# Expert weights in pieces of 1024 columns, with four gate/up buffers instead of three

## The chip, the cores and the metric

The kernel runs on one core of one Trainium2 chip. Its time is the device time of one execution in microseconds (us); lower is better. The kernel before took 1544.51 us, the median of 3 runs (1544.26 to 1546.76).

## The reference, cut to what matters

The reference is one step of a two-layer decoder trunk for a prompt of 512 rows and 64 sample rows, 576 rows of 1024 float32 columns in all. Each layer runs three token mixers, merges them, normalises (LN1), and then runs a mixture of experts and a second normalisation (LN2):

```python
D_MODEL = 1024; SEQ = 512; DEPTH = 2; DEC_BATCH = 8; DEC_SEQ = 8
N_EXPERTS = 16; N_EXPERT_GROUPS = 4; TOP_K = 2; D_EXPERT = D_MODEL // 4
# Each layer (DeepNorm post-normalisation, alpha = (2*DEPTH)^(1/4)):
#   x <- LN1(alpha*x + W_out( sum_b sigmoid(G_b x) * P_b(mixer_b(x)) ))   b in {pool, gmlp, nsa}
#   x <- LN2(alpha*x + MoE(x))     (one router shared by all layers; group-limited top-2)
'w_gate': nrm(ks[28], (DEPTH, N_EXPERTS, D_MODEL, D_EXPERT), D_MODEL ** -0.5),
'w_up':   nrm(ks[29], (DEPTH, N_EXPERTS, D_MODEL, D_EXPERT), D_MODEL ** -0.5),
'w_down': nrm(ks[30], (DEPTH, N_EXPERTS, D_EXPERT, D_MODEL), D_EXPERT ** -0.5 * DN_BETA),
```

Every row goes to two of 16 experts. An expert is a gate and an up product (1024 columns to 256 each), a gated activation, and a down product (256 to 1024). Its weights are 2 MB of gate and up (2048 KB) and 1 MB of down (1024 KB), all of them read in every layer.

## The kernel before, in words

The work that the change touches is the expert stage, `experts(k)`, once in each layer, and the end of `merge(k)` ahead of it. The rows of one expert are gathered into chunks of 128 slots. The first 16 chunks are the 16 experts: chunks 0 to 13 are written out (`STATIC = 14`), chunks 14 and up run in a loop of pairs, here one pair, so that chunks 0 to 15 are computed in each layer. A seventeenth chunk's gate/up weights are loaded and prepared but not used.

Five queues work on a chunk n, each in its own written order and bound to the others by semaphores.

- PE (lines 1807 to 1846): `gate_up(n)`, 24 matrix products of 512 columns; `hidden_t(n-1)`; `next_rows_t`, the transposes of the gathered rows of chunk n+1 (L1808); `down(n-1)`, 8 products (L1843).
- ACT: `gate_up_high(n+1)`, four copies of 1024 columns that round the raw gate/up weights to their high part (L1881); then small copies, and `output_copy(n-1)`, which moves the result of a down product to a buffer `y_a` or `y_b` (L1901, L1902).
- DVE: the low part of the same weights, written over the raw ones in place (L2036), and the hidden row.
- POOL: for each chunk an indirect DMA that gathers the rows of a later chunk into `rows_a` or `rows_b` (L1946), and one that adds the result of a chunk to the rows of the tensor `expert_rows` (L1950, here called the scatter). Two scatters may hit one row, so a scatter waits until the one before it has landed. One chunk's instructions stand as: wait for the transposes, gather (four chunks ahead of the scatter), wait for `output_copy`, wait for the scatter before, scatter. POOL's transfers go by the queue q0.
- SP: all weight loads, by the queue q1. A load of gate/up (`load_gu`, L1738) moves 128 rows of 4096 columns, 16,384 bytes each; a load of down (`load_dw`, L1741) 128 rows of 2048 columns, 8,192 bytes each. Both queues run on the same 16 DMA engines.

Three raw gate/up buffers go round (`RING_E = 3`, the number `ch.raw` of a chunk), and three for down (`ch.dslot`). SP loads gate/up of chunk n when `gate_up(n-3)` is finished, and right behind it, when `down(n-4)` is finished, the down weights of chunk n-1. The gate/up weights of the chunks 0 to 2 are issued at the end of `merge(k)` (L1425), ahead of the stores of the normalised rows (L1428, L1429); the down weights of these chunks at the beginning of the expert stage.

The functions that the diff touches, with their line numbers:

Of the kernel before, what the change touches and what calls it, by code (L numbers as in the profile page):

```python
# [14 lines left out]
F32 = mybir.dt.float32  # L15
# [12 lines left out]
KT_D = D // 128  # L28
# [56 lines left out]
def constants():  # L85
# [58 lines left out]
    put("lane", np.tile(r, (128, 1)))  # L144
    put("row1", r + 1)
    put("tile128", np.tile(128 * (np.arange(2 * NTT) % NTT), (128, 1)))
    put("pairgate", np.tile(np.where(np.arange(6) == 0, STATIC - 1, STATIC + 2 * np.arange(6)), (128, 1)))
    put("over", np.tile(128 * (15 - np.arange(16)), (128, 1)))
    spare = np.concatenate([np.zeros(MAXCH + 2), TOK + np.arange(MAXCH + 2)])
    put("pad", np.where(r[:, None] < 127, 8192, spare[None]) + 1)  # L150
# [47 lines left out]
def build(nc, io):  # L198
    with ExitStack() as ctx:
# [46 lines left out]
        for l in range(L):  # L246
            k.layer = l
            LAYER_NAME[0] = f"_{l + 1}" if l else ""
            k.dve, k.act, k.pool = Steps(nc.vector, dve_s), Steps(nc.scalar, act_s), Steps(nc.gpsimd, pool_s)
            k.merge = MergeBuffers(k)  # L250
            with ExitStack() as phase:
                def sp(name, shape, dt=F32):
                    return phase.enter_context(sbuf(nc, name, shape, dt))
                k.z = sp("z", [128, NTT, TM])
                k.qT = sp("qT", [128, GQA, SEQ])
                k.qsT = sp("qsT", [128, B, GQA, TS])
                k.KT = sp("KT", [128, 2, SEQ])
                k.KTs = sp("KT_sample", [128, 2, NS])
                k.kcT = sp("kcT", [128, NKV, 32])
                k.kcsT = sp("kcT_sample", [128, NB - 32])  # L260
                k.vblk = sp("vblk", [128, NKV, GQA, HD])
                k.vcs = sp("vcs", [128, NKV, HD])
                k.gates = sp("gates", [128, NTT, 24])
                k.gsr = sp("gates_by_row", [128, 2, NKV, 3])
                k.small = sp("small", [128, NSMALL])
                k.s = {n: k.small[:, lo:hi] for n, (lo, hi) in _S.items()}
                front(k)
            with ExitStack() as weights:
                k.gu, k.guL = two_types(nc, weights, "gate_up", [128, RING_E, 4096])
                k.dw = weights.enter_context(sbuf(nc, "down", [128, RING_E, 2048], F32))  # L270
            k.guH = [t[:, :, :].rearrange("p a t -> p (a t)")[:, 0:4096] for t in (k.oT_low, k.xT_low)]
            k.gu_in = [sem(f"gate_up_in{n}") for n in range(RING_E)]
            k.dw_in = [sem(f"down_in{n}") for n in range(RING_E)]
            k.w_hi, k.w_lo = sem("gate_up_high"), sem("gate_up_low")
            merge(k)
            experts(k)
            nums = [s.num for s in k.sems]
            assert sorted(nums) == list(range(min(nums), max(nums) + 1))

            nc.gpsimd.dma_reset(range(min(nums), max(nums) + 1))  # L280
            nc.all_engine_barrier(sems_to_clear=range(min(nums), max(nums) + 1))
# [1003 lines left out]
RING_E = 3  # L1285


PIECES = 4
PW = 4096 // PIECES
EARLY = 3  # L1290
# [77 lines left out]
def merge(k):  # L1368
# [16 lines left out]
    with ExitStack() as ctx:  # L1385
# [18 lines left out]
        @block.sync  # L1404
        def _(sp):
            for u in range(FIRST_M, NU):
                if u >= RING + FIRST_M:

                    sp.wait_ge(unit_done, u - RING + 1)
                dst = w32[:, u % RING, 0:width[u]]  # L1410
                if u < NG_:
                    sp.dma_start(dst, io["wm"][l, u // 3, :, UNIT_AT[u % 3]:UNIT_AT[u % 3 + 1]]).then_inc(w_in[u % RING], 16)
                else:
                    kk = 2 * (u - NG_)
                    sp.dma_start(dst.rearrange("p (k n) -> p k n", k=2), io["wo"][l, :, kk:kk + 2, 0:HALF]
                                 ).then_inc(w_in[u % RING], 16)

            sp.wait_ge(unit_done, NG_)
            for q in range(4):
                sp.dma_start(wo32[:, 2 * q:2 * q + 2, :], io["wo"][l, :, 2 * q:2 * q + 2, HALF:D]).then_inc(wo_in[q], 16)  # L1420
            norm.load(sp)

            sp.wait_ge(unit_done, NU)
            for n in range(RING_E):
                sp.dma_start(k.gu[:, n, :], io["we"][l, n, :, 0:4096]).then_inc(k.gu_in[n], 16)  # L1425
            for i, rows in enumerate(TILES):
                sp.wait_ge(norm.ready, 2 * i + 2)
                sp.dma_start(io["x1"][i * 128:i * 128 + rows, :], k.x[0:rows, i, :]).then_inc(x1_stored, 16)  # L1428
                sp.dma_start(io["ys"][i * 128:i * 128 + rows, :], k.x[0:rows, i, :]).then_inc(k.sum_started, 16)  # L1429

        @block.tensor
        def _(pe):
# [74 lines left out]
        def _(act):  # L1507
# [38 lines left out]
            for i in range(NTT):  # L1546
                if i == 2:

                    act.wait_ge(m_done, NTT)
                    act.wait_ge(k.gu_in[0], 16)  # L1550
                    first_expert_high(0)
                norm.copies(act, i)
                if i in (2, 3):
                    first_expert_high(i - 1)
# [87 lines left out]


def fixed_chunk(c):
    return Chunk(c, c % 2, c // 2, c % RING_E, c // RING_E + 1, c % RING_E, c % RING_E, c // RING_E + 1)


def looped_chunk(p, a):

    n, half = p * 2 + (STATIC + a), p + (STATIC + a) // 2  # L1650
    if a % 2:
        return Chunk(n, 1, half, 0, p + (a // 2 + 6), 0, 1, p + (a // 2 + 6))
    return Chunk(n, 0, half, 1, p + (a // 2 + 5), 2, 2, p + (a // 2 + 5))


def experts(k):
# [7 lines left out]
    gu, guL, guH, dw = k.gu, k.guL, k.guH, k.dw  # L1664
# [17 lines left out]
    with ExitStack() as outer:  # L1682
# [5 lines left out]
        with ExitStack() as ctx:  # L1688
# [14 lines left out]
            with ExitStack() as routing:  # L1703
# [12 lines left out]
                slotf = sr("slot_f", [128, 2, NTT])  # L1716
                sloti, lane, chunkno = (sr(n, [128, 2 * NTT], I32) for n in ("slot_i", "slot_lane_i", "slot_chunk_i"))
                C3 = sr("slot_rows", [128, 2 * NTT, 3, NTAB], BF16)
                CW3 = sr("slot_weights", [128, 2 * NTT, 3, NTAB], BF16)
# [4 lines left out]
            y = [sb("y_a", [128, D]), sb("y_b", [128, D])]  # L1724
            xTH, xTL = sb("rowsT_high", [128, KT_D, 128], F32R), sb("rowsT_low", [128, KT_D, 128], F32R)
            block = ctx.enter_context(nc.Block())

# [7 lines left out]
            @block.sync  # L1735
            def _(sp):
                def load_gu(ch, e):
                    sp.dma_start(gu[:, ch.raw, :], io["we"][l, e, :, 0:4096]).then_inc(gu_in[ch.raw], 16)  # L1738

                def load_dw(ch, e):  # L1740
                    sp.dma_start(dw[:, ch.dslot, :], io["we"][l, e, :, 4096:6144]).then_inc(dw_in[ch.dslot], 16)  # L1741
                for n in range(RING_E):
                    load_dw(fixed_chunk(n), n)
                norm.load(sp)
                for n in range(RING_E, STATIC + 1):
                    sp.wait_ge(gu_done, n - RING_E + 1)
                    load_gu(fixed_chunk(n), n)
                    if n > RING_E:
                        sp.wait_ge(dn_done, n - RING_E)
                        load_dw(fixed_chunk(n - 1), n - 1)  # L1750
                with sp.Fori(0, pairs(sp)) as p:
                    even, odd, after = looped_chunk(p, 0), looped_chunk(p, 1), looped_chunk(p, 2)
                    e = [sp.value_load(plan[0:1, bass.ds(ch.n, 1)], min_val=0, max_val=E - 1) for ch in (even, odd, after)]
                    gate = sp.value_load(plan[0:1, bass.ds(p + 34, 1)], min_val=STATIC - 1, max_val=STATIC + 10)

                    sp.wait_ge(gu_done, gate)
                    load_gu(odd, e[1])
# [18 lines left out]
            def _(pe):  # L1776
# [39 lines left out]
                def gate_up(ch):  # L1816
                    out = ps[:, GB + ch.side, :]
                    for kk in range(KT_D):
# [7 lines left out]
                        last = pe.matmul(out, xTH[:, kk, :], guL[:, ch.slot, cols], start=False, stop=(kk == KT_D - 1))  # L1826
                    last.then_inc(gu_done, 1)

                def hidden_t(ch):
# [5 lines left out]
                def down(ch, first=False):  # L1835
# [1 line left out]

                        pe.wait_ge(y_out, ch.n)
                    pe.wait_ge(ht_out, ch.n + 1)
                    pe.wait_ge(dw_in[ch.dslot], ch.d_nth * 16)  # L1840
# [27 lines left out]
            def _(act):  # L1868
# [3 lines left out]
                act.activation(ex[0:NS, NT, :], ps[0:NS, LOGITS, NT * E:NTT * E], ACT.Exp, scale=-1.0).then_inc(ex_ready, 1)  # L1872

                def gate_up_high(ch, early=False, begin=0):
                    act.wait_ge(gu_in[ch.raw], ch.raw_nth * 16)
                    if not early:

                        act.wait_ge(gu_done, ch.n - 1)
                    for q in range(begin, PIECES):
                        cols = slice(q * PW, (q + 1) * PW)  # L1880
                        act.copy(guH[ch.side][:, cols], gu[:, ch.raw, cols]).then_inc(w_hi, 1)  # L1881

                def rows_high(count):
                    act.wait_ge(xt_done, count)
# [104 lines left out]
            def _(dve):  # L1989
# [42 lines left out]
                def gate_up_low(ch, pieces=(0, 1, 2, 3)):  # L2032
                    for q in pieces:
                        cols = slice(q * PW, (q + 1) * PW)
                        dve.wait_ge(w_hi, ch.n * PIECES + (q + 1))
                        dve.tensor_tensor(guL[:, ch.slot, cols], gu[:, ch.raw, cols], guH[ch.side][:, cols].bitcast(F32),  # L2036
                                          ALU.subtract).then_inc(w_lo, 1)


# [366 lines left out]
```

## Time and profile before

| what | value |
|---|---|
| median of 3 runs | 1544.51 us |
| the profiled execution's own time | 1547.95 us |
| its span, first to last instruction | 1546.3 us |
| mean granted TensorE clock | 0.963 |
| PE busy | 1432.9 us (93%) |
| DVE, ACT, POOL busy | 800.9, 612.4, 171.3 us |
| DMA moved | 239.75 MB, mean 155 GB/s |
| expert stage of the first layer | about 560 to 745 us |
| expert stage of the second layer | about 1323 to 1506 us |

Durations and places come from the profiled execution; it lies 3.44 us above the median of the runs. A busy share is the time in which an engine had an instruction; a DMA share is the time in which its 16 engines had packets. PEclk is the clock that TensorE was granted, as a part of full speed. In timelines the first number is the start in us from the beginning of the span, the second the duration, and a bracket gives the idle time ahead of the instruction and what ended it.

### The profile page before, as it was taken

What the parts mean: (1) busy time and instruction counts of PE and PEld (TensorE: products, weight loads), DVE (VectorE), ACT (ScalarE), POOL (GpSimd) and SP (SyncE); (2) the same over time, 40 slices, a digit from 0 to 9 for tenths busy, and PEclk for the clock granted to TensorE, in tenths of its full rate; (3) what the DMA queues carried; (4) which work ended last, traced back from release to release, by engine and by line L of the source; (5) the groups of instructions that cost most, each with busy time, mean ns of one, the idle gap of its engine ahead of it and who ended that gap; (6) DMA issues with size and microseconds to landing.
All of it is one profiled execution on the core that took longest, in us unless ns stands there. A gap on an engine that the chain in (4) does not pass through costs nothing. (4 is left out here: it accounts for less than half of the span.)

```text
span 1546.3 us, 23017 instructions
## 1 busy us (share of the span) xinstructions
PE 1432.9 (93%) x9168; PEld 1166.6 (75%) x9168; DVE 800.9 (52%) x1351; ACT 612.4 (40%) x1156; POOL 171.3 (11%) x152
## 2 busy tenths in 40 slices
PE   7999899999999959989799999999999998799895
PEld 6897665999997846656478966669999976566563
DVE  3224767433333766656842257673333347766565
ACT  3322578322222226656323326772222212465550
POOL 3012000000000112222112210000000001122230
PEclk9999899999999969999899999999999998799997
DMA  8334400322223759997423143021222256599953
GB/s 269 87 124 159 143 2 2 110 80 85 89 69 109 286 187 334 341 317 268 143 109 120 56 169 134 2 76 56 89 75 90 65 202 244 203 342 341 326 173 125
DMA packets 55861, 239.75 MB, mean 155 GB/s; under 512 B 11718, under 2 KB 19796, under 8 KB 45964
## 3 DMA queue, kind: packets, MB, share of 16 engines
q1 hardware_dynamic: 44716, 216.08, 39.0%
q0 software_dynamic: 11040, 22.21, 6.0%
q8 instruction: 73, 1.20, 0.3%
q14 instruction: 32, 0.26, 0.1%
HBM read 224.55 MB, written 34.49 MB: 168 GB/s over the span
## 5 line engine op out<-in xcount | busy, mean ns | idle before, releaser
L1435 PE MATMUL ps<-xT_high,w_high 128*128 128x288 f32 x704 | 208.0, 295 | 0.0
L1436 PE MATMUL ps<-xT_low,w_high 128*128 128x288 f32 x704 | 207.2, 294 | 0.0
L1437 PE MATMUL ps<-xT_high,w_ring_low 128*128 128x288 f32 x704 | 206.3, 293 | 0.0
L1533 ACT ACTIVATE tanh_gate<-ps 128x576 f32<-128x576 f32 x48 | 31.3, 652 | 295.8 <-PE ps L1437 295.8
L1437 PEld LDWEIGHTS ps<-xT_high,w_ring_low 128*128 128x128 f32 x704 | 132.6, 188 | 0.0
L1436 PEld LDWEIGHTS ps<-xT_low,w_high 128*128 128x128 f32 x704 | 132.5, 188 | 0.0
L1435 PEld LDWEIGHTS ps<-xT_high,w_high 128*128 128x128 f32 x704 | 132.1, 188 | 0.0
L1843 PE MATMUL ps<-down,hidT 128*128 128x512 f32 x256 | 118.0, 604 | 4.2 <-ACT hidT L1894 2.4
L1585 DVE SCALAR_TENSOR_TENSOR branch_part<-tanh_gate,ps 128x576 f32<-128x576 f32 x32 | 24.1, 754 | 176.5 <-ACT tanh_gate L1533 176.5
L1327 POOL TENSOR_TENSOR ln_rs<-ln_mv,const 128x1 f32<-128x1 f32 (+1 forms) x20 | 17.5, 873 | 868.7 <-DVE ln_mv L1322 868.7
L557 PE MATMUL ps<-z_w_high_part,oT_low 128*128 128x454 f32 x260 | 97.3, 374 | 8.7 <-DVE z_w_ring_low L1041 8.7
L2036 DVE TENSOR_TENSOR gate_up_low<-gate_up,oT_low 128x1024 fp32r<-128x1024 f32 x66 | 76.5, 1219 | 55.2 <-ACT oT_low L1881 55.2
L1826 PE MATMUL ps<-gate_up_low,rowsT_high 128*128 128x512 f32 x256 | 102.7, 401 | 0.0
L1041 DVE TENSOR_TENSOR z_w_ring_low<-z_w_ring,z_w_high_part 128x908 fp32r<-128x908 f32 (+1 forms) x34 | 34.1, 1006 | 123.1 <-ACT z_w_high_part L871 122.9
L558 PE MATMUL ps<-z_w_ring_low,oT_low 128*128 128x454 f32 x260 | 96.8, 372 | 0.0
L559 PE MATMUL ps<-z_w_high_part,xT_low 128*128 128x454 f32 x260 | 96.8, 372 | 0.0
L2036 DVE TENSOR_TENSOR gate_up_low<-gate_up,xT_low 128x1024 fp32r<-128x1024 f32 x64 | 74.1, 1218 | 43.8 <-ACT xT_low L1881 43.5
L1560 DVE TENSOR_TENSOR w_ring_low<-w_ring,w_high 128x1280 fp32r<-128x1280 f32 (+2 forms) x52 | 79.7, 1533 | 20.4 <-ACT w_high L1517 19.0
L1843 PEld LDWEIGHTS ps<-down,hidT 128*128 128x128 f32 x256 | 47.2, 195 | 52.7 <-issue 52.6
L963 ACT ACTIVATE probs<-ps,row_max 128x128 f32<-128x128 f32 (+4 forms) x152 | 78.7, 532 | 17.8 <-DVE row_max L1182 17.6
L1182 DVE TENSOR_REDUCE row_max<-ps 128x2 f32<-128x1024 f32 (+3 forms) x76 | 60.6, 800 | 41.6 <-PE ps L723 30.2
L1517 ACT CAST w_high<-w_ring 128x1280 fp32r<-128x1280 f32 (+2 forms) x52 | 67.2, 1292 | 15.9 <-PE ps L1437 9.7
(368 smaller groups left out, 3314.5 us busy)
## 6 DMA issues: line engine op xcount, KB each, us to landing
gate_up<-in_we SPq DMA_DIRECT2D x34, 2048.0 KB, 12.2
down<-in_we SPq DMA_DIRECT2D x32, 1024.0 KB, 10.2
w_ring<-in_wm SPq DMA_DIRECT2D x28, 640.0 KB, 4.1
z_w_ring<-in_wtm SPq DMA_DIRECT2D x30, 454.0 KB, 4.1
w_ring<-in_wm SPq DMA_DIRECT2D x16, 768.0 KB, 4.5
w<-in_w SPq DMA_DIRECT2D x2, 2048.0 KB, 8.8
sel_pages<-in_sel_pages SPq DMA_DIRECT2D x32, 128.0 KB, 2.0
win_rows<-in_win_rows SPq DMA_DIRECT2D x2, 2048.0 KB, 8.1
```

Of the source, the lines that this page charges most:

```text
L557: pe.matmul(out, w[0], x[0], start=first, stop=False)
L558: pe.matmul(out, w[0], x[1], start=False, stop=False)
L559: return pe.matmul(out, w[1], x[0], start=False, stop=last)
L963: act.activation(P[:, m % 3, h, 0:w], ps[:, bank + h, 0:w], ACT.Exp, bias=mx[:, m % 3, h:h + 1], accum_out=den[:, m % 3, h:h + 1]).then_in ...
L1435: pe.matmul(out, w[0], x[0], start=first, stop=False)
L1436: pe.matmul(out, w[0], x[1], start=False, stop=False)
L1437: return pe.matmul(out, w[1], x[0], start=False, stop=last)
L1517: act.copy(wh[:, u % HRING, 0:width[u]], w32[:, u % RING, 0:width[u]]).then_inc(w_hi, 1)
L1560: return dve.tensor_tensor(low, src, high.bitcast(F32), ALU.subtract)
L1826: last = pe.matmul(out, xTH[:, kk, :], guL[:, ch.slot, cols], start=False, stop=(kk == KT_D - 1))
L1843: last = pe.matmul(ps[:, YB + n, :], hT[:, f, :], dw[:, ch.dslot, f * D + n * 512:f * D + (n + 1) * 512], start=(f == 0), stop=(f == 1))
L2036: dve.tensor_tensor(guL[:, ch.slot, cols], gu[:, ch.raw, cols], guH[ch.side][:, cols].bitcast(F32), ALU.subtract).then_inc(w_lo, 1)
```

## The change

Every load of expert weights is cut into DMAs of 1024 columns, so that a row of a DMA is 4096 bytes: four DMAs for gate/up, two for down, on the same semaphore, whose waits are for four or two times 16. There is a fourth raw gate/up buffer, `gate_up_d`, and a chunk's buffer is its number modulo four (in the loop 3 and 0 in turn). Gate/up of chunk n is loaded when `gate_up(n-4)` is finished, one chunk earlier than before, and chunk 3's at the end of `merge(k)`, after the stores of the fourth row tile. Down weights still go round three buffers and wait for the same `down`; in SP's order they stand one chunk later relative to gate/up.

```diff
-    put("pairgate", np.tile(np.where(np.arange(6) == 0, STATIC - 1, STATIC + 2 * np.arange(6)), (128, 1)))
+    put("pairgate", np.tile(np.where(np.arange(6) == 0, STATIC - 2, STATIC + 2 * np.arange(6)), (128, 1)))
...
+                weights.enter_context(sbuf(nc, "below_gate_up_d", [128, 8264], F32))
+                fourth, fourth_low = two_types(nc, weights, "gate_up_d", [128, 4096])
+            k.raw = [k.gu[:, n, :] for n in range(RING_E)] + [fourth[:, :]]
+            k.low = [k.guL[:, n, :] for n in range(RING_E)] + [fourth_low[:, :]]
...
+RING_G = 4
+GU_COLS = [slice(n * 1024, (n + 1) * 1024) for n in range(4)]
+DOWN_COLS = [slice(n * 1024, (n + 1) * 1024) for n in range(2)]
+GU_LOADED, DOWN_LOADED = 16 * len(GU_COLS), 16 * len(DOWN_COLS)
...
             for n in range(RING_E):
-                sp.dma_start(k.gu[:, n, :], io["we"][l, n, :, 0:4096]).then_inc(k.gu_in[n], 16)
+                for cols in GU_COLS:
+                    sp.dma_start(k.gu[:, n, cols], io["we"][l, n, :, cols]).then_inc(k.gu_in[n], 16)
             for i, rows in enumerate(TILES):
...
+                if i == NTT - 2:
+                    for cols in GU_COLS:
+                        sp.dma_start(k.raw[3][:, cols], io["we"][l, 3, :, cols]).then_inc(k.gu_in[3], 16)
...
 def fixed_chunk(c):
-    return Chunk(c, c % 2, c // 2, c % RING_E, c // RING_E + 1, c % RING_E, c % RING_E, c // RING_E + 1)
+    return Chunk(c, c % 2, c // 2, c % RING_G, c // RING_G + 1, c % RING_G, c % RING_E, c // RING_E + 1)
...
     if a % 2:
-        return Chunk(n, 1, half, 0, p + (a // 2 + 6), 0, 1, p + (a // 2 + 6))
-    return Chunk(n, 0, half, 1, p + (a // 2 + 5), 2, 2, p + (a // 2 + 5))
+        return Chunk(n, 1, half, 3, p + (a // 2 + 4), 3, 1, p + (a // 2 + 6))
+    return Chunk(n, 0, half, 0, p + (a // 2 + 4), 2, 2, p + (a // 2 + 5))
...
                 def load_gu(ch, e):
-                    sp.dma_start(gu[:, ch.raw, :], io["we"][l, e, :, 0:4096]).then_inc(gu_in[ch.raw], 16)
+                    for cols in GU_COLS:
+                        sp.dma_start(gu[ch.raw][:, cols], io["we"][l, e, :, cols]).then_inc(gu_in[ch.raw], 16)
...
-                for n in range(RING_E, STATIC + 1):
-                    sp.wait_ge(gu_done, n - RING_E + 1)
+                for n in range(RING_G, STATIC + 1):
+                    sp.wait_ge(gu_done, n - RING_G + 1)
                     load_gu(fixed_chunk(n), n)
-                    if n > RING_E:
-                        sp.wait_ge(dn_done, n - RING_E)
-                        load_dw(fixed_chunk(n - 1), n - 1)
+                    if n > RING_G:
+                        sp.wait_ge(dn_done, n - RING_G)
+                        load_dw(fixed_chunk(n - 2), n - 2)
+                sp.wait_ge(dn_done, STATIC - 3)
+                load_dw(fixed_chunk(STATIC - 1), STATIC - 1)
```

SP's order, at the end of `merge(k)` and the beginning of the expert stage of the first layer, before (L1425 and L1738 load gate/up, L1741 down; L1428 and L1429 store the last, 64-row tile):

```order
L1425 DMA gate_up<-in_we 128x4096 [waits unit_done]
L1425 DMA gate_up<-in_we 128x4096 x2
...
L1428 DMA x1_rows<-x 64x1024 [waits ln1_ready]
L1429 DMA expert_rows<-x 64x1024
...
L1741 DMA down<-in_we 128x2048 x3
L1312 DMA ln2_gb<-in_ln 128x2048
L1738 DMA gate_up<-in_we 128x4096 [waits gate_up_done] x2
L1741 DMA down<-in_we 128x2048 [waits down_done]
```

and now (L1438, L1445 and L1757 load gate/up, L1761 down):

```order
L1438 DMA gate_up<-in_we 128x1024 [waits unit_done]
L1438 DMA gate_up<-in_we 128x1024 x11
...
L1445 DMA gate_up_d<-in_we 128x1024 x4
L1441 DMA x1_rows<-x 64x1024 [waits ln1_ready]
L1442 DMA expert_rows<-x 64x1024
...
L1761 DMA down<-in_we 128x1024 x6
L1324 DMA ln2_gb<-in_ln 128x2048
L1757 DMA gate_up<-in_we 128x1024 [waits gate_up_done]
L1757 DMA gate_up<-in_we 128x1024 x3
```

Three loads have become twelve, and four for the fourth buffer stand ahead of the last tile's stores; the first load of the expert stage, which waits for the same first `gate_up`, is now that of chunk 4 instead of chunk 3.

SP's order at the end of the written-out chunks, before the loop's plan is read, before:

```order
L1738 DMA gate_up<-in_we 128x4096 [waits gate_up_done]
L1741 DMA down<-in_we 128x2048 [waits down_done]
L1738 DMA gate_up<-in_we 128x4096 [waits gate_up_done]
L1741 DMA down<-in_we 128x2048 [waits down_done]
L1733 TENSOR_LOAD plan [waits plan_ready]
```

and now:

```order
L1757 DMA gate_up<-in_we 128x1024 [waits gate_up_done]
L1757 DMA gate_up<-in_we 128x1024 x3
L1761 DMA down<-in_we 128x1024 [waits down_done]
L1761 DMA down<-in_we 128x1024
L1761 DMA down<-in_we 128x1024 [waits down_done]
L1761 DMA down<-in_we 128x1024
L1751 TENSOR_LOAD plan [waits plan_ready]
```

The down weights of chunk 13 stand by themselves at the end, since no gate/up load is left in front of them.

## Rows read from the trace of the kernel before

**Rows 1.** Busy time of each engine in two stretches, first layer.

```profile
core 0: us, PE busy (x) PEld busy (x) DVE busy (x) ACT busy (x) POOL busy (x), PEclk, DMA share, GB/s
596.00:637.00 41.00, 41.00 (x171) 28.53 (x170) 26.90 (x32) 26.39 (x40) 8.84 (x6) 1.00 0.98 353
640.00:692.00 52.00, 46.28 (x188) 31.83 (x187) 28.27 (x34) 27.44 (x43) 13.76 (x9) 0.97 0.93 320
```

**Rows 2.** Timeline of PE: transposes of gathered rows, both layers.

```profile
581.90 1.04 PE L1808 MATMUL ps<-const,rows_a 128*128 128x128 f32 x8
592.04 1.04 PE L1808 MATMUL ps<-const,rows_b 128*128 128x128 f32 x8
...
654.78 1.09 PE L1808 MATMUL ps<-const,rows_b 128*128 128x128 f32 x8 [1.65 <-DMA rows_b<-x_rows,slot_table]
...
733.77 1.04 PE L1808 MATMUL ps<-const,rows_a 128*128 128x128 f32 x8
...
1344.07 1.04 PE L1808 MATMUL ps<-const,rows_a 128*128 128x128 f32 x8
...
1498.14 1.04 PE L1808 MATMUL ps<-const,rows_a 128*128 128x128 f32 x8
```

**Rows 3.** Waits of PE's weight loads, 560 to 740 us: total, times, longest.

```profile
PEld ps L1808 <- DMA rows_b<-x_rows,slot_table: 4.7, 3, 2.4
PEld ps L1808 <- DMA rows_a<-x_rows,slot_table: 2.8, 2, 2.1
```

**Rows 4.** Timeline of POOL: scatters (L1950) and a gather (L1946), first layer.

```profile
637.83 1.59 POOL L1950 DMA_INDIRECT expert_rows<-y_a,slot_table  x1 [9.04 <-DMA expert_rows<-y_b,slot_table]
...
649.76 1.59 POOL L1950 DMA_INDIRECT expert_rows<-y_b,slot_table  x1 [8.49 <-DMA expert_rows<-y_a,slot_table]
651.65 1.54 POOL L1946 DMA_INDIRECT rows_a<-x_rows,slot_table  x1 [0.31 <-issue]
...
708.70 1.59 POOL L1950 DMA_INDIRECT expert_rows<-y_a,slot_table  x1 [9.46 <-DMA expert_rows<-y_b,slot_table]
...
716.72 1.59 POOL L1950 DMA_INDIRECT expert_rows<-y_b,slot_table  x1 [4.60 <-DMA expert_rows<-y_a,slot_table]
```

**Rows 5.** DMA queues (packets, MB, share) and a load, 640 to 692 us.

```profile
q1 hardware_dynamic: 1327, 14.11, 71.0%
q0 software_dynamic: 1251, 2.52, 22.3%
...
gate_up<-in_we SPq DMA_DIRECT2D x5, 2048.0 KB, 13.9
```

**Rows 6.** DMA queues, 742 to 746 us, then q0 from 1505 to 1509 us.

```profile
q1 hardware_dynamic: 193, 0.62, 41.9%
q0 software_dynamic: 207, 0.28, 37.0%
...
q0 software_dynamic: 288, 0.28, 47.7%
```

**Rows 7.** Queue q1 in 502:512, 739:742 and 380:490 us; page's issue row.

```profile
q1 hardware_dynamic: 237, 3.62, 90.3%
...
q1 hardware_dynamic: 310, 1.01, 91.5%
...
q1 hardware_dynamic: 3472, 10.88, 30.5%
...
w_ring<-in_wo SPq DMA_DIRECT2D x8, 512.0 KB, 3.7
```

**Rows 8.** Timeline of SP's issues, first layer.

```profile
642.68 0.33 SPq L1738 DMA_DIRECT2D gate_up<-in_we  x1
647.34 0.33 SPq L1741 DMA_DIRECT2D down<-in_we  x1
...
718.73 0.33 SPq L1738 DMA_DIRECT2D gate_up<-in_we  x1
```

**Rows 9.** Timeline of ACT at the last chunk, first layer.

```profile
728.64 0.59 ACT L1902 COPY y_b<-ps 128x512 f32<-128x512 f32 x1
730.44 3.89 ACT L1881 CAST oT_low<-gate_up 128x1024 fp32r<-128x1024 f32 x4 [1.21 <-DMA gate_up<-in_we]
```

More of the change, by code:

```diff
@@ L270, in build @@
                 k.dw = weights.enter_context(sbuf(nc, "down", [128, RING_E, 2048], F32))
+                weights.enter_context(sbuf(nc, "below_gate_up_d", [128, 8264], F32))
+                fourth, fourth_low = two_types(nc, weights, "gate_up_d", [128, 4096])
+            k.raw = [k.gu[:, n, :] for n in range(RING_E)] + [fourth[:, :]]
+            k.low = [k.guL[:, n, :] for n in range(RING_E)] + [fourth_low[:, :]]
             k.guH = [t[:, :, :].rearrange("p a t -> p (a t)")[:, 0:4096] for t in (k.oT_low, k.xT_low)]
-            k.gu_in = [sem(f"gate_up_in{n}") for n in range(RING_E)]
+            k.gu_in = [sem(f"gate_up_in{n}") for n in range(RING_G)]
             k.dw_in = [sem(f"down_in{n}") for n in range(RING_E)]
@@ L1549, in _ @@
                     act.wait_ge(m_done, NTT)
-                    act.wait_ge(k.gu_in[0], 16)
+                    act.wait_ge(k.gu_in[0], GU_LOADED)
                     first_expert_high(0)
@@ L1663, in experts @@
     gu_in, dw_in, w_hi, w_lo = k.gu_in, k.dw_in, k.w_hi, k.w_lo
-    gu, guL, guH, dw = k.gu, k.guL, k.guH, k.dw
+    gu, guL, guH, dw = k.raw, k.low, k.guH, k.dw
     idx_ready, x_in = sem("idx_ready"), [sem("rows_in_a"), sem("rows_in_b")]
@@ L1718, in experts @@
                 C3 = sr("slot_rows", [128, 2 * NTT, 3, NTAB], BF16)
+                sr("under_gate_up_d", [128, 4104])
                 CW3 = sr("slot_weights", [128, 2 * NTT, 3, NTAB], BF16)
@@ L1724, in experts @@
             y = [sb("y_a", [128, D]), sb("y_b", [128, D])]
+            sb("over_gate_up_d", [128, 4096])
             xTH, xTL = sb("rowsT_high", [128, KT_D, 128], F32R), sb("rowsT_low", [128, KT_D, 128], F32R)
@@ L1737, in load_gu @@
                 def load_gu(ch, e):
-                    sp.dma_start(gu[:, ch.raw, :], io["we"][l, e, :, 0:4096]).then_inc(gu_in[ch.raw], 16)
+                    for cols in GU_COLS:
+                        sp.dma_start(gu[ch.raw][:, cols], io["we"][l, e, :, cols]).then_inc(gu_in[ch.raw], 16)
                 def load_dw(ch, e):
-                    sp.dma_start(dw[:, ch.dslot, :], io["we"][l, e, :, 4096:6144]).then_inc(dw_in[ch.dslot], 16)
+                    for cols in DOWN_COLS:
+                        sp.dma_start(dw[:, ch.dslot, cols], io["we"][l, e, :, 4096 + cols.start:4096 + cols.stop]
+                                     ).then_inc(dw_in[ch.dslot], 16)
                 for n in range(RING_E):
@@ L1753, in _ @@
                     e = [sp.value_load(plan[0:1, bass.ds(ch.n, 1)], min_val=0, max_val=E - 1) for ch in (even, odd, after)]
-                    gate = sp.value_load(plan[0:1, bass.ds(p + 34, 1)], min_val=STATIC - 1, max_val=STATIC + 10)
+                    gate = sp.value_load(plan[0:1, bass.ds(p + 34, 1)], min_val=STATIC - 2, max_val=STATIC + 10)
                     sp.wait_ge(gu_done, gate)
@@ L1825, in gate_up @@
                         pe.matmul(out, xTL[:, kk, :], guH[ch.side][:, cols], start=False, stop=False)
-                        last = pe.matmul(out, xTH[:, kk, :], guL[:, ch.slot, cols], start=False, stop=(kk == KT_D - 1))
+                        last = pe.matmul(out, xTH[:, kk, :], guL[ch.slot][:, cols], start=False, stop=(kk == KT_D - 1))
                     last.then_inc(gu_done, 1)
@@ L1839, in down @@
                     pe.wait_ge(ht_out, ch.n + 1)
-                    pe.wait_ge(dw_in[ch.dslot], ch.d_nth * 16)
+                    pe.wait_ge(dw_in[ch.dslot], ch.d_nth * DOWN_LOADED)
                     for n in range(2):
@@ L1874, in gate_up_high @@
                 def gate_up_high(ch, early=False, begin=0):
-                    act.wait_ge(gu_in[ch.raw], ch.raw_nth * 16)
+                    act.wait_ge(gu_in[ch.raw], ch.raw_nth * GU_LOADED)
                     if not early:
@@ L1880, in gate_up_high @@
                         cols = slice(q * PW, (q + 1) * PW)
-                        act.copy(guH[ch.side][:, cols], gu[:, ch.raw, cols]).then_inc(w_hi, 1)
+                        act.copy(guH[ch.side][:, cols], gu[ch.raw][:, cols]).then_inc(w_hi, 1)
                 def rows_high(count):
@@ L2035, in gate_up_low @@
                         dve.wait_ge(w_hi, ch.n * PIECES + (q + 1))
-                        dve.tensor_tensor(guL[:, ch.slot, cols], gu[:, ch.raw, cols], guH[ch.side][:, cols].bitcast(F32),
+                        dve.tensor_tensor(guL[ch.slot][:, cols], gu[ch.raw][:, cols], guH[ch.side][:, cols].bitcast(F32),
                                           ALU.subtract).then_inc(w_lo, 1)
```

## The prediction

> **What bounds the kernel now.** I read the busy time of the expert stage first, then PE's timeline, its waits, POOL's timeline, and last the DMA queues. In the stretch from 596 to 637 us PE is busy all of the time at full clock; from 640 to 692 us it is busy for 46.28 of 52 us and its granted clock is 0.97 [rows 1]. So the first half of the stage is bound by PE, and the second half is not. The pace of a chunk where PE is full is 592.04 - 581.90 = 10.14 us. From the transposes at 581.90 to those at 733.77 there are 14 chunks: 151.87 us, where 14 x 10.14 = 141.96 would do. The first layer loses 9.9 us. In the second layer 1498.14 - 1344.07 = 154.07, a loss of 12.1 us [rows 2]. Together that is 22.0 us, and it is all that a change of the waits in this stretch can win.
>
> PE loses it on the gathers: the transposes wait for rows_b three times and for rows_a twice, 7.5 us in the first layer [rows 3]; the rest is matrix work at a lower clock after such a wait. The gathers come late because POOL is late. It waits 8.5 to 9.5 us for the scatter before, then issues scatter and gather within 3.5 us and waits again. From the scatter at 637.83 to that at 708.70 there are six cycles of 11.8 us, longer than PE's 10.14 [rows 4]. Each cycle adds some 1.7 us to POOL's lag, and after five or six of them the gather has used up its lead. The scatter at 708.70 was over in 8.0 us, when the lagging PE had let the weight loads run dry [rows 4].
>
> What makes a cycle long is in the queues. In the 52 us, q0 (gathers and scatters) moved 2.52 MB, 0.0485 MB per us, beside q1 (weights) with 14.11 MB in 1327 packets [rows 5]. A cycle of 11.8 us moves 0.57 MB by q0; to do this in 10.14 us it needs 0.056 MB per us.
>
> **The change part by part.** *Pieces of 4096 bytes.* The nearest row for q0 beside small packets is the stretch from 742 to 746 us, where q1 loads z_w_ring in rows of 3632 bytes (454 KB over 128). There q0 moved 0.28 MB in 4 us, 0.07 MB per us, a scatter alone, the slower of the two kinds. With nothing on q1 a scatter moved the same 0.28 MB in 4 us [rows 6]. So beside small packets q0 was as fast as alone, beside the large ones 0.69 of it. I take 0.07: a cycle is 0.57 / 0.07 = 8.1 us, under 10.14. POOL then waits for PE and no longer the other way, and both losses go: -22.0 us. From the other side, q0 stays at 0.0485: 0 us. The stretch at 742 has q1 at 41.9% only, so it is not a full load; I still take it, since q1 was full just ahead of it (91.5% from 739 to 742) [rows 7].
>
> The Trainium skill says in "DMA: Bandwidth & Descriptors", section "Queues, rings and completion order", that a DMA engine goes round between the queues it has work for, a whole packet at a time. By that rule q0's turn comes sooner with shorter weight packets; the rows above bear this out, and no term here is taken from it.
>
> *What the pieces cost the weights.* A chunk's weights are 3.146 MB (2048 + 1024 KB). Time of the 16 engines per MB: in large packets alone 9.03 us / 3.62 MB = 2.49, in 3632-byte packets 2.745 / 1.01 = 2.72, in the merge stage, where loads come one by one, 33.6 / 10.88 = 3.08 [rows 7]; in large packets beside q0 36.9 / 14.11 = 2.62 [rows 5]. A chunk is then 7.8, 8.6, 9.7 and 8.2 us. q0 adds 11.6 us over 4.4 cycles, 2.6 us a chunk. The sum is 10.4 to 12.3 us, against a pace of 10.14: at full pace the DMA engines are slightly overbooked, by 1.1 us a chunk at the value that I take, 8.6 + 2.6 = 11.2.
>
> *The fourth buffer* pays for this. A load is issued when a gate_up ends (642.68); ACT uses it one pace and then 4.66 us (to the end of the down product, 647.34) and two copies of 0.59 later [rows 8, 9], 15.9 us in all, and it landed in 13.9 [rows 5]. Now it is issued one pace earlier, so the lead is 2.0 + 10.1 = 12.1 us. Over the 12 chunks from 4 to 15 the overbooking sums to 12 x 1.1 = 13.2 us; 1.1 us a layer is left, at 10.4 us a chunk nothing, at 12.3 us 13.8. I take 1 us a layer: +2.0 us.
>
> *The end of the stage.* The weights of chunk 16, which nobody uses, are issued behind the down product of chunk 12, now as before. They landed 11.7 us after 718.73, and ACT waited 1.21 us for them ahead of the last hidden row [rows 8, 9]. The change brings no lead here, and PE's pace ahead of it is shorter. Landing may come some us later or, with q1 emptied by the earlier loads, sooner: -1 to +3 us a layer; I take +0.5, so +1.0 us.
>
> *Issues.* A chunk has six DMAs instead of two, four more of 0.33 us [rows 8], 1.3 us of SP in 10.14: hidden behind SP's waits for PE. If SP were late, the fourth buffer's lead covers it. At the end of merge nine more issues are some 3 us and stand ahead of stores that wait for their normalised tile. The four for the fourth buffer stand ahead of the last tile's stores; 2 MB at the above rates are 5 us, and what reads those stores is a gather that first waits for the slot table. I cost them at nothing; uncovered, it would be 5 us a layer. The down weights wait for the same down product as before: nothing.
>
> Sum: -22.0 + 2.0 + 1.0 = -19 us. From the profiled execution's 1547.95 that is 1528.95; the median of the runs lies 3.44 lower: 1525.5 us, and -19 is put on it.
>
> **The rivals.** *Part of it (A).* q0 gets faster, and the weights become the bound. If the price of 2.72 grows beside q0 as that of the large packets did (2.49 to 2.62), a chunk is 9.0 + 2.6 = 11.6 us; 12 x 1.46 - 12.1 = 5.4 us a layer are lost again. Speaks for it: the DMA share is 0.98 already at full pace [rows 1]. Against: part of q0's share was time spent beside large packets. Time: 1544.5 - 22 + 10.8 + 1 = 1534.
>
> *The scatter stays slow (B).* It lasts as long beside 4096-byte packets as beside 16384-byte ones, because full DMA engines and not long packets hold it up. POOL's cycle remains near 11.8 us and the fourth buffer helps nobody, since PE waits for gathers and not for weights. For it: the share of 0.93 to 0.98. Against: rows 6. Time: 1544.5, give or take 3.
>
> *The pieces slow the weights down (C), the side on which the kernel gets slower.* With the merge stage's price, 9.7 + 2.6 = 12.3 us a chunk: 12 x 2.16 - 12.1 = 13.8 us a layer, against 11 lost now, and the last loads come later too, some 2 us a layer. Time: 1544.5 + 2 x (13.8 - 11 + 2) = 1554. It decides from 12 us a chunk, that is, when the weights flow below some 335 GB/s while q0 works. Against it: that row holds the starts of loads that come singly.
>
> *One piece after the other (D).* If each of the six DMAs had to be over before the next flows, each would be 3.7 us, as a 512 KB load alone is [rows 7]: 22.2 + 2.6 us a chunk, 12 x 14.7 - 12.1 = 164 us a layer instead of 11, 1850 us. Four such loads flowed at 91.5% from 739 to 742 us, which speaks against it [rows 7]. The Trainium skill has a rule of this kind: in the section "Bandwidth" of the same page it wants at least 1 MiB a DMA, since each has a fixed cost of about 2 us. By its fit (an estimate: 2.0 us and bytes over 436 GB/s) a piece would be 3.2 us, and the kernel would take about 1780 us. The trace does not agree for loads issued back to back.
>
> **How the numbers follow.** The forecast as told, 1519 to 1530 us: 0.60. Better than that, since the clock never falls and the last wait goes too: 0.03. A: 0.17. B: 0.10. C: 0.09. D: 0.01. Within 0.2%, 3 us, is about what a measurement of this kernel can't tell from no change. Faster takes the forecast, the better case, A and a little of B: 0.81. No change is most of B: 0.07. Slower is the rest of B, C and D: 0.12. The range from 1517 to 1545 us takes in the forecast, A and half of B; C, D and a rest are left out. The forecast's own range is 1519 to 1530.
>
> **What would show it.** If the steps are right, PE's transposes wait for no gather, they come every 10.14 us to the end, and the clock stays at 1.00; POOL waits for PE's transposes or ACT's copies, its cycle is 10.14 us, and q0 moves more than 0.056 MB per us beside q1. Gate/up loads land later than 13.9 us after their issue, up to 24, and no copy of ACT waits for them but that of chunk 16. A shows ACT waiting for gate_up at chunks 12 to 15. B shows POOL's wait of 8.5 us for the scatter again. C shows A's waits and a DMA share near 1.0 at under 335 GB/s of weights. I am wrong if the scatter's time doesn't depend on the length of the weight packets, or if the shorter ones cost the weights more than the fourth buffer's lead.

## The result, and the profile after

The changed kernel takes 1537.96 us, the median of 15 runs (1533.91 to 1547.86), where the kernel before took 1546.33 us (15 runs): a ratio of 0.9943, 95% interval 0.9930 to 0.9957. That is 8.4 us less; 19 had been forecast. Its profiled execution took 1536.7 us (span 1535.0), against 1547.95 and 1546.3.

The transposes of PE (L1831, before L1808) show where the time is. They answer to [rows 2]; the first number is the start.

```profile
579.34 1.04 PE L1831 MATMUL ps<-const,rows_a 128*128 128x128 f32 x8
589.47 1.04 PE L1831 MATMUL ps<-const,rows_b 128*128 128x128 f32 x8
...
700.84 1.04 PE L1831 MATMUL ps<-const,rows_a 128*128 128x128 f32 x8
712.00 1.04 PE L1831 MATMUL ps<-const,rows_b 128*128 128x128 f32 x8
728.53 1.04 PE L1831 MATMUL ps<-const,rows_a 128*128 128x128 f32 x8
...
1337.27 1.04 PE L1831 MATMUL ps<-const,rows_a 128*128 128x128 f32 x8
...
1486.97 1.04 PE L1831 MATMUL ps<-const,rows_a 128*128 128x128 f32 x8
```

For twelve chunks the pace holds: 700.84 - 579.34 = 121.50, 10.13 us each. Then come 11.16 and 16.53 us. Over the same 14 chunks as before, 728.53 - 579.34 = 149.19 us is 7.2 over 14 x 10.14 = 141.96, and in the second layer 149.70 is 7.7 over it. Before it was 9.9 and 12.1. So 22.0 us of loss have become 15.0; the remaining 4.3 us by which the spans differ lie outside these stretches, 2.6 of them ahead of the first; nothing shows that they belong to the change.

The stretches themselves answer to [rows 1]: PE's busy time (the first pair after the length), and behind the five engines PEclk, DMA share and GB/s.

```profile
596.00:637.00 41.00, 41.00 (x172) 28.70 (x171) 27.38 (x33) 26.89 (x42) 12.36 (x8) 1.00 1.00 348
640.00:692.00 52.00, 52.00 (x222) 36.51 (x220) 34.82 (x42) 33.60 (x52) 14.52 (x11) 1.00 0.97 325
...
712.00:730.00 18.00, 13.54 (x54) 8.92 (x53) 11.43 (x13) 11.06 (x16) 6.51 (x7) 0.91 0.68 212
```

From 640 to 692 us PE is now busy all the time, at full clock. The idle time has moved to the end, and the clock falls there, to 0.91. No transpose waits for a gather any more. POOL's scatters (L1973), which answer to [rows 4], show why:

```profile
638.50 1.86 POOL L1973 DMA_INDIRECT expert_rows<-y_b,slot_table  x1 [5.68 <-DMA expert_rows<-y_a,slot_table]
641.88 1.04 POOL L1969 DMA_INDIRECT rows_a<-x_rows,slot_table  x1 [1.52 <-PE ps L1831]
648.60 1.86 POOL L1973 DMA_INDIRECT expert_rows<-y_a,slot_table  x1 [5.68 <-DMA expert_rows<-y_b,slot_table]
...
691.28 1.96 POOL L1973 DMA_INDIRECT expert_rows<-y_a,slot_table  x1 [6.80 <-DMA expert_rows<-y_b,slot_table]
```

The wait for the scatter before is 5.7 to 7.3 us; in [rows 4] it was 8.5 to 9.5. From 638.50 to 691.28 there are five cycles of 10.6 us in the mean, where there were six of 11.8 (five of 11.9 to 13.5, and one of 7.8). In the first two POOL has time to wait for PE, later no more: 10.6 us is still longer than PE's 10.13.

What ends PE's run is in ACT's timeline, at the copies of chunk 15's gate/up weights, first layer and second:

```profile
713.12 3.88 ACT L1904 CAST xT_low<-gate_up_d 128x1024 fp32r<-128x1024 f32 x4 [5.66 <-DMA gate_up_d<-in_we]
```

```profile
1471.75 3.88 ACT L1904 CAST xT_low<-gate_up_d 128x1024 fp32r<-128x1024 f32 x4 [5.35 <-DMA gate_up_d<-in_we]
```

The next thing in ACT's order is the hidden row for which the down product waits, so PE stands still behind it. SP issued that load here (answers to [rows 8]; the second number is the time of the whole group of four issues):

```profile
640.05 2.30 SPq L1757 DMA_DIRECT2D gate_up_d<-in_we  x4
...
660.31 6.31 SPq L1757 DMA_DIRECT2D gate_up<-in_we  x4
...
670.45 7.21 SPq L1757 DMA_DIRECT2D gate_up<-in_we  x4
...
689.45 3.14 SPq L1757 DMA_DIRECT2D gate_up_d<-in_we  x4
```

From 689.45 to the end of ACT's wait at 713.12 are 23.7 us. The queues from 640 to 692 us answer to [rows 5]; below them are those from 596 to 637 and from 700 to 705 us.

```profile
q1 hardware_dynamic: 3837, 13.96, 72.1%
q0 software_dynamic: 1427, 2.92, 24.1%
...
gate_up<-in_we SPq DMA_DIRECT2D x12, 512.0 KB, 14.7
...
rows_a<-x_rows,slot_table POOLq DMA_INDIRECT x3, 9.5
```

```profile
q1 hardware_dynamic: 3233, 11.77, 76.0%
q0 software_dynamic: 1171, 2.46, 24.1%
```

```profile
q1 hardware_dynamic: 194, 0.71, 34.7%
q0 software_dynamic: 128, 0.29, 20.4%
```

The last pair was the riddle. ACT's wait for chunk 15's weights runs from 707.46 to 713.12 us. Just ahead of it, some ten us after their issue, when they are still on their way, the 16 engines are busy for only 55% of the time, and weights flow at 0.71 MB in 5 us. (During the wait itself the share is 0.93 again, since SP issues chunk 16's load at 708.02.) A mean of about one half, while something is late, can mean that one half of the engines works and the other half has nothing left.

The packets' own start and duration in the trace say the same. Taken every 0.01 us from 700 to 705 us, never fewer than 7 packets are under way, and 7 to 9 of them, most often 8, in 87% of the samples. In the kernel with spread rows below, from 640 to 680 us, there are never fewer than 13, mostly 16 or 17.

### The profile page after: what moved, and what is told of

It reads as the page before. It is cut to its first block and busy times, and to the rows that moved or that the text cites. A ratio compares the mean times of both kernels' runs of the same rounds, so it can differ in the third digit from the quotient of the medians.

```text
span 1535.0 us, 23185 instructions
## 1 busy us (share of the span) xinstructions
PE 1429.1 (93%) x9168; PEld 1163.6 (76%) x9168; DVE 800.8 (52%) x1351; ACT 613.7 (40%) x1156; POOL 172.7 (11%) x152
## 5 line engine op out<-in xcount | busy, mean ns | idle before, releaser
L1866 PE MATMUL ps<-down,hidT 128*128 128x512 f32 x256 | 119.0, 608 | 14.0 <-ACT hidT L1917 11.6
L1601 DVE SCALAR_TENSOR_TENSOR branch_part<-tanh_gate,ps 128x576 f32<-128x576 f32 x32 | 24.1, 754 | 175.6 <-ACT tanh_gate L1549 175.6
L1849 PE MATMUL ps<-gate_up_low,rowsT_high 128*128 128x512 f32 x192 | 77.3, 403 | 0.0
L984 ACT COPY probsT<-ps 128x128 f32<-128x128 f32 (+3 forms) x152 | 57.2, 427 | 37.0 <-PE ps L767 31.0
```

Source lines behind the costliest of these rows:

```text
L1849: last = pe.matmul(out, xTH[:, kk, :], guL[ch.slot][:, cols], start=False, stop=(kk == KT_D - 1))
L1866: last = pe.matmul(ps[:, YB + n, :], hT[:, f, :], dw[:, ch.dslot, f * D + n * 512:f * D + (n + 1) * 512], start=(f == 0), stop=(f == 1))
```

## The experiments

Three theories of the 15 us that remain, before the first runs:

- **H**: the rows of q0 lie on one half of the DMA engines. A chunk has 128 slots, filled from the first; 576 rows x 2 experts / 16 = 72 of them are used in the mean, on partitions 0 to 71. If the partition decides which engine moves a row, one half of the engines carries nearly all of q0 beside its share of the weights, and a load is over only when the slowest engine is.
- **M**: the 16 engines are overbooked as a whole, as the prediction reckoned, only by more.
- **O**: SP issues chunk 15's load too late, behind the down weights and the reading of the plan.

The Trainium skill, "DMA: Bandwidth & Descriptors", section "The descriptor swizzle", says that in a transfer to 128 partitions partitions 0 to 63 are written by engines 0 to 7 and partitions 64 to 127 by engines 8 to 15, in groups of four neighbouring partitions. It says it of one plain transfer that writes them; whether an indirect one that skips slots, or the scatter, which reads them, is spread likewise, the runs below had to tell. By it 64 of the 72 rows would lie on eight engines.

**Pieces alone.** The changed kernel with three gate/up buffers and the old order of the loads:

```diff
-    return Chunk(c, c % 2, c // 2, c % RING_G, c // RING_G + 1, c % RING_G, c % RING_E, c // RING_E + 1)
+    return Chunk(c, c % 2, c // 2, c % RING_E, c // RING_E + 1, c % RING_E, c % RING_E, c // RING_E + 1)
...
-                for n in range(RING_G, STATIC + 1):
-                    sp.wait_ge(gu_done, n - RING_G + 1)
+                for n in range(RING_E, STATIC + 1):
+                    sp.wait_ge(gu_done, n - RING_E + 1)
```

> Loads in pieces of 1024 columns, but three gate/up buffers and the order of before. Three theories for the 5.7 us that ACT waits for the gate/up weights of chunk 15 in the changed kernel. H: the rows that are gathered and added lie on half of the 16 DMA engines, so those are overbooked by some 1.6 us a chunk. M: the DMA engines as a whole are overbooked, 10.8 us of work a chunk against 10.14. O: SP issues chunk 15's load too late. All: POOL's cycle falls from 11.8 us to PE's pace, as in the changed kernel. H: with a lead of 2 us instead of 12, ACT waits for weights at many chunks, 12 x 1.6 - 2 = 17 us a layer, 12 us slower than before (1558). M and O: 12 x 0.7 - 2 = 6 us a layer, 1537.

Measured: 1552.6 us (5 runs), ratio to before 1.0039, 1.0022 to 1.0057: slower than before. H had 1558, M and O 1537; it is nearer to H, and 5 us under it. The 14 chunks lose 14.2 and 14.4 us. ACT's waits from 560 to 740 us (total, times, longest):

```profile
ACT oT_low L1890 <- DMA gate_up<-in_we: 13.3, 5, 3.6
ACT xT_low L1890 <- DMA gate_up<-in_we: 11.2, 5, 3.2
```

The weights are late ten times in the first layer. So with pieces the weights come late, and the fourth buffer is what turns the change into a gain: the two together lose 15.0 us, the pieces alone 28.6. Whether the pieces themselves are dearer or q0 takes its turns from them, this run doesn't tell.

**The buffer alone.** The changed kernel with whole loads:

```diff
-GU_COLS = [slice(n * 1024, (n + 1) * 1024) for n in range(4)]
-DOWN_COLS = [slice(n * 1024, (n + 1) * 1024) for n in range(2)]
+GU_COLS = [slice(0, 4096)]
+DOWN_COLS = [slice(0, 2048)]
```

> Four gate/up buffers and the new order, but loads in one piece as before (16384 and 8192 bytes a row). All theories: POOL's cycle stays near 11.8 us, PE waits for gathers as before, about 7.5 us in the first layer, and the time is that of before, 1546, within 3 us. If the length of the weight packets did not matter, it would be that of the changed kernel, 1538.

Measured: 1542.66 us (10 runs), ratio 0.9981, 0.9956 to 1.0006. PE still waits for gathers, as in [rows 3]; waits from 560 to 745 us:

```profile
PEld ps L1831 <- DMA rows_b<-x_rows,slot_table: 4.6, 2, 2.7
...
PEld ps L1831 <- DMA rows_a<-x_rows,slot_table: 2.6, 2, 1.9
```

The losses are 8.6 and 7.7 us. It is the short packets that free the gathers, not the buffer. (The losses are still 5.7 us under those of before. 3.4 us of that are shorter gather waits in the second layer, 6.4 us instead of 9.8; why, stays open.)

**The rows spread over all partitions.** The changed kernel, with slot 32 d + w on partition 4 w + d, so that the 72 rows lie on every group of four partitions. Only the comparison that makes the one-hot table of slots is changed:

```diff
-                    dve.tensor_tensor(R[:, a * NTT:(a + 1) * NTT, :],
+                    dve.tensor_tensor(R[:, a * NTT:(a + 1) * NTT, :].rearrange("p i (w d) -> p i w d", d=4),
...
-                                      c["lane"].unsqueeze(1).broadcast_to([128, NTT, 128]), ALU.is_equal).then_inc(lanes_ready, 1)
+                                      c["lane"].rearrange("p (d w) -> p w d", d=4).unsqueeze(1).broadcast_to([128, NTT, 32, 4]),
+                                      ALU.is_equal).then_inc(lanes_ready, 1)
```

> The changed kernel, with the slots of a chunk placed so that slots 0 to 31 lie on every fourth partition, the next 32 beside them, and so on; a chunk has some 72 rows of 128, which then lie over all partitions and not on the first 72. H: q0's work is the same on all DMA engines, 10.8 us a chunk on each, 12 x 0.7 = 8 us under the lead of 12; SP's issues no longer stall for microseconds, ACT doesn't wait for chunk 15's weights, the first layer's transposes keep 10.14 us to the end, and the time falls by 11 to 15 us against the changed kernel, to 1525. M and O: nothing changes, 1538, ACT waits 5 us and more at chunk 15.

Measured: 1526.34 us (4 runs), ratio 0.9883, 0.9858 to 0.9907. The 14 chunks take 141.76 us in both layers: nothing is lost. Here is the first layer's stretch:

```profile
577.83 1.04 PE L1831 MATMUL ps<-const,rows_a 128*128 128x128 f32 x8
...
719.59 1.03 PE L1831 MATMUL ps<-const,rows_a 128*128 128x128 f32 x8
```

The queues from 640 to 692 us:

```profile
q1 hardware_dynamic: 3955, 14.41, 71.9%
q0 software_dynamic: 1548, 3.08, 25.0%
...
gate_up<-in_we SPq DMA_DIRECT2D x12, 512.0 KB, 7.0
```

The engines work as much in the mean (71.9% and 25.0%, against 72.1% and 24.1%), and the loads land in 7.0 us instead of 14.7. M falls: the mean was never too much.

**The same spreading in the kernel before.** The same edit, with neither pieces nor fourth buffer.

> The kernel before (one piece, three buffers), with the slots of a chunk spread over all partitions as in the run above. H: each DMA engine has about half as many rows of a gather or scatter to take in turn with the large weight packets, so POOL's cycle falls from 11.8 us below 10.14, and PE no longer waits for gathers; with a lead of 2 us the weights are late instead by up to 6 us a layer: 1537, or 1526 if they are not. M and O: POOL's cycle stays at 11.8 us and the time at 1546.

Measured: 1528.86 us (4 runs), ratio 0.9904, 0.9877 to 0.9931. It loses 0.8 us in the first layer and nothing in the second. The queues from 640 to 692 us, against [rows 5]:

```profile
q1 hardware_dynamic: 1465, 15.90, 77.6%
q0 software_dynamic: 1511, 3.05, 23.3%
...
gate_up<-in_we SPq DMA_DIRECT2D x5, 2048.0 KB, 9.7
```

Beside the long packets q0 moved 3.05 MB in 52 us, 0.059 MB per us, where it had moved 0.0485. Where the rows lay was worth more than the whole change.

**A block, turned by 32 and by 64 partitions.** Spreading also makes used and skipped slots take turns in a DMA's list; call it K that this was the gain. These two keep the rows in one block. In the first it lies on partitions 32 to 103, on both halves; in the second on 64 to 127 and 0 to 7, again on one half. Here for 32:

```diff
-                    dve.tensor_tensor(R[:, a * NTT:(a + 1) * NTT, :],
-                                      lane[:, a * NTT:(a + 1) * NTT].unsqueeze(2).broadcast_to([128, NTT, 128]),
-                                      c["lane"].unsqueeze(1).broadcast_to([128, NTT, 128]), ALU.is_equal).then_inc(lanes_ready, 1)
+                    for to, of in ((slice(32, 128), slice(0, 96)), (slice(0, 32), slice(96, 128))):
+                        last = dve.tensor_tensor(R[:, a * NTT:(a + 1) * NTT, to],
+                                                 lane[:, a * NTT:(a + 1) * NTT].unsqueeze(2).broadcast_to([128, NTT, to.stop - to.start]),
+                                                 c["lane"][:, of].unsqueeze(1).broadcast_to([128, NTT, to.stop - to.start]), ALU.is_equal)
+                    last.then_inc(lanes_ready, 1)
```

> The changed kernel with the slots of a chunk turned by 32 partitions (slot s on partition (s + 32) mod 128), still in one contiguous block. H (half of the 16 DMA engines carry q0's rows): the rows of a chunk, about 72, now lie on partitions 32 to 103, that is on both halves, so the time is that of the spread rows, 1526 (1521 to 1530), transposes every 10.13 us to the end and no wait for chunk 15's gate/up. Rival K (the gain of the spread rows came from rows and skipped slots taking turns in a DMA's list, not from where they lie): a contiguous block is as slow as before, 1538 (1534 to 1541), with ACT's wait for chunk 15 of about 5 us.

> The same edit, turned by 64 partitions: the rows lie on partitions 64 to 127 and 0 to 7, so again on one half of the engines, the other one. H: 1538 (1534 to 1541) as the changed kernel, ACT waits some 5 us for chunk 15's gate/up in each layer. K: 1538 too. If it was not the share of a half, but that the first 64 partitions' engines have other work, or that the edit itself is quicker: about 1526.

Measured: turned by 32, 1523.3 us (6 runs), ratio 0.9844, 0.9804 to 0.9885; turned by 64, 1542.48 us (11 runs), ratio 0.9960, 0.9936 to 0.9984. The same instructions but for the widths of those comparisons, and 19 us between them. (H had 1534 to 1541 for the second, and ACT waits of some 5 us, which are 3.6 and 3.9.) The losses are 0 and 1.4 us against 9.8 and 8.0. The first layer's stretch, SP's issue of chunk 15's load and ACT's copy of it, turned by 32:

```profile
579.13 1.04 PE L1831 MATMUL ps<-const,rows_a 128*128 128x128 f32 x8
...
720.89 1.04 PE L1831 MATMUL ps<-const,rows_a 128*128 128x128 f32 x8
```

```profile
660.11 1.83 SPq L1757 DMA_DIRECT2D gate_up<-in_we  x4
...
689.30 2.00 SPq L1757 DMA_DIRECT2D gate_up_d<-in_we  x4
```

```profile
706.14 3.89 ACT L1904 CAST xT_low<-gate_up_d 128x1024 fp32r<-128x1024 f32 x4
```

and turned by 64:

```profile
579.21 1.04 PE L1831 MATMUL ps<-const,rows_a 128*128 128x128 f32 x8
...
730.97 1.04 PE L1831 MATMUL ps<-const,rows_a 128*128 128x128 f32 x8
```

```profile
660.19 6.93 SPq L1757 DMA_DIRECT2D gate_up<-in_we  x4
...
690.68 4.36 SPq L1757 DMA_DIRECT2D gate_up_d<-in_we  x4
```

```profile
715.55 1.05 ACT L1904 CAST xT_low<-gate_up_d 128x1024 fp32r<-128x1024 f32 x1 [3.60 <-DMA gate_up_d<-in_we]
```

Turned by 32, the load goes out at 689.30, only 0.15 us earlier than in the changed kernel, and ACT doesn't wait for it. So O falls as well: SP's order issues the load early enough. (In the second layer ACT did wait for it there, 2.55 us; that is the 1.4 us.) K falls too. The first half of the partitions isn't special either: the other half alone is as bad. By the rule of the Trainium skill a block on partitions 32 to 103 has 32 rows on the one half and 40 on the other; the runs agree with it for indirect transfers, as far as the two halves go. Which engine moved a row no run shows. Whether it is the engine itself or its way into the buffer that fills up, the profile doesn't tell either, since it doesn't name the engine of a packet.

**The parts again, with the rows spread.**

> Pieces of 1024 columns, three gate/up buffers and the old order, with rows spread over all 16 engines. H: the mean DMA work is 10.8 us a chunk against 10.14, 0.7 x 12 = 8 us a layer against a lead of 2 us if the mean counts; if the weights alone get quicker where no engine is behind, nothing is late: 1527 to 1538, 15 to 25 us under the same kernel with unspread rows (1552.6). M (engines overbooked as a whole): within 4 us of 1552.

> Whole loads of 4096 and 2048 columns, four gate/up buffers and the new order, with rows spread. H: no wait for gathers is left and none for weights, 1526 to 1530, equal to the changed kernel with spread rows within 3 us, since neither the length of the packets nor the buffer is needed then. Rival: the short packets still bring q0's turn sooner, which is worth 6 us or more: 1533 or above here.

The edits are those above, added up. Measured: pieces without the fourth buffer 1522.54 us (6 runs), ratio 0.9839, 0.9809 to 0.9868; the buffer without pieces 1525.15 us (7 runs), ratio 0.9841, 0.9813 to 0.9870. Both keep the pace of 10.13 us through all 14 chunks of both layers. The pieces that cost 6 us with the rows on one half cost nothing here. For pieces that is under H's range of 1527 to 1538, whose upper part reckoned the 16 engines overbooked by 0.7 us a chunk. They were not, as the queues of pieces with three buffers from 640 to 692 us show:

```profile
q1 hardware_dynamic: 4405, 16.04, 79.9%
q0 software_dynamic: 1441, 2.95, 22.5%
...
gate_up<-in_we SPq DMA_DIRECT2D x21, 512.0 KB, 6.8
```

At PE's full pace, with a lead of 2.0 us, the loads landed in 6.8 us, so no backlog grew. The two shares add up to 102.4%: packets overlap on an engine there, and a price in engine time that is worked out from such shares comes out too high.

The five versions with rows on both halves lie between 1522.5 and 1528.9 us; these runs can't order them. All of them have a better ratio than the changed kernel, though for the kernel before with spread rows the two intervals just touch (0.9877 to 0.9931, 0.9930 to 0.9957). The experiments ran on two chips, on which the kernel before took 1546.7 and 1547.7 us; each ratio is to the runs of its own chip.

| rows of a chunk | loads | gate/up buffers | loss over 14 chunks, layers 1 and 2 | median, us |
|---|---|---|---|---|
| on one half | whole | 3 (before) | 9.9, 12.1 | 1546.3 |
| on one half | pieces | 3 | 14.2, 14.4 | 1552.6 |
| on one half | whole | 4 | 8.6, 7.7 | 1542.7 |
| on one half | pieces | 4 (after) | 7.2, 7.7 | 1538.0 |
| on the other half | pieces | 4 | 9.8, 8.0 | 1542.5 |
| turned by 32 | pieces | 4 | 0, 1.4 | 1523.3 |
| spread | pieces | 4 | 0, 0 | 1526.3 |
| spread | whole | 3 | 0.8, 0 | 1528.9 |
| spread | pieces | 3 | 0, 0 | 1522.5 |
| spread | whole | 4 | 0, 0 | 1525.2 |

## Why the prediction was right in direction and wrong in size

**The gather waits, -22.0 us: right in what it won, for this layout; the rate was too high.** No transpose waits for a gather. But q0 moved 2.92 MB in 52 us beside full weight loads, 0.0562 MB per us, where 0.07 had been taken, from a stretch with the weights at 41.9%. So POOL's cycle is 10.6 us and not 8.1, and POOL still waits for the scatter before. Such a cycle moves 0.0562 x 10.6 = 0.59 MB, so that 10.13 us would need 0.0585, not 0.056: POOL still falls back by 0.4 us a chunk. That PE doesn't feel it in 16 chunks is due to the gathers, which are issued early and land sooner, in 9.5 us. Before it was

```profile
rows_a<-x_rows,slot_table POOLq DMA_INDIRECT x2, 14.9
```

in the same stretch. The runs with whole loads say that it was the packets: the buffer alone left the waits.

**"The fourth buffer pays for this", +2.0 us: the step that failed.** It measured 15.0. The step reckoned the 16 engines as one, overbooked by 11.2 - 10.14 = 1.1 us a chunk, so that 13.2 us stood against a lead of 12.1. The shares of the changed kernel give nearly that price: 76.0% of 41 us for 11.77 MB is 2.65 us per MB, 8.3 us a chunk; q0 took 24.1% of 41 us over 4.05 chunks, 2.4 us; 10.8 together. But as one they were not overbooked at all: with the rows on both halves and a lead of only 2.0 us, pieces lost nothing, where 1.1 us a chunk would have cost 11 us a layer. What was late was one half. A load has landed when its last row has, and the half that carries q0's rows is behind. How far can be read twice: with a lead of 12.1 us the loss was 7.2 to 7.7, so (12.1 + 7.4) / 12 = 1.6 us a chunk; with three buffers, a lead of 2.0 and a loss of 14.3, (2.0 + 14.3) / 12 = 1.4. So the late half needs 11.5 to 11.8 us a chunk. That the forecast's 1.1 lies so near is chance. If 64 of 72 rows lie on that half, as the rule of the Trainium skill cited above has it, an estimate from the same rows is 8.3 + 2.4 x 2 x 64/72 = 12.6 us, which would lose 17 us a layer: too much. Part of the 1 us between may be the prices, which come out too high from such shares; the rest stays open.

**The end of the stage, +1.0 us: no cost seen.** From the last transposes to the end of the span it was 1546.3 - 1498.14 = 48.2 us before and 1535.0 - 1486.97 = 48.0 after.

**Issues, nothing: right in effect, wrong in the reason.** Four issues were to be 1.3 us; in the second half they took up to 7.2. From 660 to 678 us SP had next to no slack in them. But the time went when the rows were turned by 32 (1.83 us where it was 6.31), so it is a sign of the late half and not a cause.

**The rivals.** A, the weights become the bound at 11.6 us a chunk and 1534 us, came closest: its sign in the trace (ACT waiting for gate/up at chunk 15), nearly its time, and its price a chunk. Its reason, a higher price per MB beside q0, was not it: the weights cost 2.65 us per MB, less than the small packets' 2.72 in [rows 7], where A needs 9.0 / 3.146 = 2.86. B and D are out: the scatters got shorter, and pieces flowed back to back. (The fit that D's paragraph takes from the Trainium skill stands in "DMA: Bandwidth & Descriptors" in the section "Anatomy of one DMA — SWDGE (gpsimd) path", for DMAs that GpSimd issues; SP issues these loads, so it priced D only by analogy.) C, the side on which the kernel gets slower, asks for 12.3 us a chunk with the fourth buffer; the late half needed 11.5 to 11.8. Pieces alone came near C's time, 1552.6 us, but with a lead of 2.0 us.

The sum as measured in the two stretches: -22.0 + 15.0 + 0 = -7.0 us; the medians show -8.4.

The row in the profile that should have raised the question was [rows 1], with [rows 5]: a load of 2 MB took 13.9 us to land, while its share of all engines' time is 2.1 x 2.62 = 5.5 us. A transfer that takes 2.5 times its own work, in a stretch where buffers keep few loads in flight, may be waiting for its slowest engine; with the rows spread it took 9.7.

## What to carry to other kernels

A mean busy share of 16 DMA engines hides which of them is late; where transfers with skipped or few rows run beside full ones, ask on which partitions the rows lie, and place them so that both halves (below and from partition 64) carry the same. Test that first, by turning the rows by 32 partitions: it is one comparison in the code, and here it was worth about 15 us on the changed kernel, more than smaller packets and another buffer together. A deeper buffer only postpones a steady deficit: with 1.4 to 1.6 us a chunk, the ten us of lead that it added were used up before the sixteenth chunk.

## What the runs showed of the hardware that was not expected

- The place of some 72 rows among 128 partitions decided 19 us of 1523 (turned by 32 against turned by 64), at equal bytes.
- Pieces of 512 KB, issued back to back, cost little more engine time than whole loads of 2 MB, by the shares: from 640 to 692 us 2.69 us per MB against 2.62 [rows 5], from 596 to 637 us 2.65 against 2.55 (77.2% of 41 us for 12.41 MB).
- With four buffers, an issue on SP took some 0.5 us with the rows on both halves (1.75 to 2.72 for four, first layer), and up to 1.8 us (7.21 for four) with them on one, late in the stage. With three buffers and the rows on one half, four issues from 580 to 705 us took 1.75 to 3.47 us. So a long queue on a late half goes with it; what holds SP up is not shown.
